# Seven-product weight chunks in the swiglu stages from chunk 3 on instead of chunk 4

## What is computed

```python
D_MODEL = 1024; SEQ = 512; DEPTH = 2; D_FF = 2816

def swiglu_ffn(x, wi, wo):
    gate, up = jnp.split(x @ wi, 2, axis=-1)
    return (jax.nn.silu(gate) * up) @ wo

for l in range(DEPTH):
    x = layer_norm(alpha * x + 0.5 * swiglu_ffn(x, ffn1_wi[l], ffn1_wo[l]), ln_g[l, 0], ln_b[l, 0])
    mix = even_mixer(x, ...) if l % 2 == 0 else odd_mixer(x, ...)
    x = layer_norm(alpha * x + mix, ln_g[l, 1], ln_b[l, 1])
    x = layer_norm(alpha * x + 0.5 * swiglu_ffn(x, ffn2_wi[l], ffn2_wo[l]), ln_g[l, 2], ln_b[l, 2])
```

## Time and profile before

| | before |
|---|---|
| median of 3 runs | 3608.43 us (3606.93 to 3611.15) |
| profiled execution, its own time | 3602.56 us |
| its span, first to last instruction | 3600.8 us |
| TensorE busy | 3516.6 us, 98% |
| VectorE busy | 2192.2 us, 61% |
| ScalarE busy | 1556.2 us, 43% |
| GpSimd busy | 476.4 us, 13% |
| mean granted TensorE clock | 0.994 |

### The profile page before, as it was taken

How to read it: one execution, slowest core, us unless ns; L and a number is a source line. 1 busy time by engine, 2 the same in 40 slices (tenths; PEclk the granted TensorE clock), 3 DMA queues, 4 the chain that set the end, 5 groups by cost and what they waited for, 6 DMA issues and landing times. The chain is left out here.

```text
span 3600.8 us, 55748 instructions
## 1 busy us (share of the span) xinstructions
PE 3516.6 (98%) x21468; PEld 3045.0 (85%) x21468; DVE 2192.2 (61%) x3419; ACT 1556.2 (43%) x2472; POOL 476.4 (13%) x443
## 2 busy tenths in 40 slices
PE   8999999999999999989999999999999999999998
PEld 7998877998899888678998887878888878888887
DVE  6963566895489445655895445656662545556643
ACT  4542544553355343543554333445442323454432
POOL 1022103002300230032102201011111000021110
PEclk9999999999999999999999999999999999999999
DMA  3232221233322322121223333222222333132222
GB/s 141 105 127 96 89 82 66 99 105 119 115 101 106 119 99 94 67 83 48 95 104 124 111 111 120 88 97 92 95 86 97 128 108 115 64 112 94 93 92 84
DMA packets 66513, 357.45 MB, mean 99 GB/s; under 512 B 7185, under 2 KB 16929, under 8 KB 37409
## 3 DMA queue, kind: packets, MB, share of 16 engines
q1 hardware_dynamic: 62368, 342.45, 26.8%
q0 software_dynamic: 3968, 12.59, 1.1%
HBM read 341.37 MB, written 13.63 MB: 99 GB/s over the span
## 5 line engine op out<-in xcount | busy, mean ns | idle before, releaser
L394 DVE TENSOR_TENSOR w_lo<-raw,w_hi 128x2048 fp32r<-128x2048 f32 (+2 forms) x233 | 482.5, 2071 | 600.6 <-ACT w_hi L389 584.6
L389 ACT ACTIVATE w_hi<-raw 128x2048 fp32r<-128x2048 f32 (+2 forms) x224 | 373.5, 1668 | 700.3 <-PE bank L432 596.5
L430 PE MATMUL bank<-x_hi,w_hi 128*128 128x512 f32 (+1 forms) x1344 | 522.6, 389 | 2.0 <-DVE w_lo L394 2.0
L431 PE MATMUL bank<-x_lo,w_hi 128*128 128x512 f32 (+1 forms) x1344 | 510.8, 380 | 0.0
L432 PE MATMUL bank<-x_hi,w_lo 128*128 128x512 f32 (+1 forms) x1344 | 510.7, 380 | 0.0
L430 PE MATMUL banks<-x_hi,w_hi 128*128 128x512 f32 (+1 forms) x832 | 323.5, 389 | 18.2 <-POOL x_lo L628 10.9
L431 PE MATMUL banks<-x_lo,w_hi 128*128 128x512 f32 (+1 forms) x832 | 318.0, 382 | 0.0
L432 PE MATMUL banks<-x_hi,w_lo 128*128 128x512 f32 (+1 forms) x832 | 317.8, 382 | 0.0
L430 PEld LDWEIGHTS bank<-x_hi,w_hi 128*128 128x128 f32 x1344 | 253.6, 189 | 64.5 <-issue 15.4
L430 PE MATMUL bank<-f_g_hi,w_hi 128*128 128x512 f32 (+1 forms) x792 | 294.2, 371 | 3.3 <-POOL f_g_lo L1338 3.3
L432 PEld LDWEIGHTS bank<-x_hi,w_lo 128*128 128x128 f32 x1344 | 253.5, 189 | 48.1
(11 more groups left out here) (595 smaller groups left out, 8326.4 us busy)
## 6 DMA issues: line engine op xcount, KB each, us to landing
raw<-in_weights SPq DMA_DIRECT2D x217, 1024.0 KB, 4.8
raw<-in_weights SPq DMA_DIRECT2D x96, 704.0 KB, 4.0
X<-x_kept SPq DMA_DIRECT2D x5, 2048.0 KB, 9.6
x_kept<-X SPq DMA_DIRECT2D x6, 1024.0 KB, 4.7
raw<-in_weights SPq DMA_DIRECT2D x8, 768.0 KB, 4.3
odd_arena<-in_kv SPq DMA_DIRECT2D x8, 512.0 KB, 3.6
x_kept<-X SPq DMA_DIRECT2D x2, 2048.0 KB, 12.7
work<-in_rpb POOLq DMA_DIRECT2D x12, 256.0 KB, 3.0
```

The source lines that it names most:

```text
L389: act.activation(w_hi[:, s, 0:size], raw[:, s, 0:size], ACT.Copy).then_inc(hi_ready.sem, 1)
L394: dve.tensor_tensor(w_lo[:, s, 0:size], raw[:, s, 0:size], w_hi[:, s, 0:size].bitcast(F32), ALU.subtract).then_inc(lo_ready.sem, 1)
L430: pe.matmul(out, wh[:, w], hi(k), start=first and n == 0, stop=False, skip_group_check=not group)
L431: pe.matmul(out, wh[:, w], lo(k), start=False, stop=False, skip_group_check=not group)
```

## The change

`S0` goes from 4 to 3: chunk 3 of each swiglu stage becomes a block chunk and is no longer split and multiplied whole. The block parts change slots and PSUM sides with it (`u` of the first block chunk is 1). The hand-written start is arranged anew on ScalarE and VectorE: the low parts of the first block chunk stand between those of T, and the combinations q = 1, 2, 3 of the first block chunk between its last low parts (`begun=True` leaves them out of `body`). Chunks 4 and 5 move partly into the loops, which begin one step earlier. In the last chunk, all seven parts go to one slot with a simpler rule, and three high parts are made ahead of the half silus.

```diff
-                S0, LATE = 4, 10
+                S0, LATE = 3, 10
-                LAST_SLOT = (3, 0, 1, 2, 3, 0, 1)
...
                 def weight_block(w, j, q):
-                    if is_last(j):
-                        return w[:, other, LAST_SLOT[q] * 512:LAST_SLOT[q] * 512 + 512]
                     at = q % 4 * 512
-                    return w[:, own if q < 4 else other, at:at + 512]
+                    return w[:, other if q < 4 or isinstance(j, int) and j == FT - 1 else own, at:at + 512]
...
-                            if j == 3:
-                                pe.wait_ge(product_ready.sem, product_ready.at(1))
...
                         gate_up(1, 0)
-                        gate_up(1, 1)
-                        blocks_of(S0, 0)
-                        blocks_of(S0 + 1, 1)
-                        with pe.Fori(3, FT // 2 - 1) as i:
+                        blocks_of(S0, 1)
+                        with pe.Fori(2, FT // 2 - 1) as i:
...
                             if j is S0:
-                                act.wait_ge(chunk_used.sem, PRIME + n0 + (3 if q < 4 else 4))
-                            elif is_last(j):
-                                if q >= 4:
-                                    act.wait_ge(block_used.sem, used_of(j, q - 4))
-                                elif q == 3:
-                                    act.wait_ge(chunk_used.sem, j + (PRIME + n0))
-                                elif q > 0:
-                                    act.wait_ge(block_used.sem, used_of(j - 1, q + 3))
+                                act.wait_ge(chunk_used.sem, PRIME + n0 + (2 if q < 4 else 3))
+                            elif isinstance(j, int) and j == FT - 1 and q >= 4:
+                                act.wait_ge(block_used.sem, used_of(j, q - 4))
...
-                        def body(j, u, v, early, more=True):
+                        def body(j, u, v, early, more=True, begun=False):
                             for q in range(7):
-                                combine(j, u, q, g)
+                                if not (begun and q < 4):
+                                    combine(j, u, q, g)
                                 block_low(j + 1, v, q)
...
                         rest(0, 1)
-                        split(1, 0)
...
-                        sums(S0, 0, range(4))
+                        sums(S0, 1, range(3))
                         low_g(0, 0)
-                        t_split(3, 1)
+                        block_low(S0, 1, 0)
+                        t_split(2, 1)
+                        block_low(S0, 1, 1)
                         t_split(1, 2)
+                        block_low(S0, 1, 2)
+                        t_split(3, 3)
+                        block_low(S0, 1, 3)
+                        sums(S0, 1, (3,))
+                        t_split(4, 5)
+                        block_low(S0, 1, 4)
                         rest(1, 0)
+                        combine(S0, 1, 1, None)
+                        block_low(S0, 1, 5)
+                        combine(S0, 1, 2, None)
+                        block_low(S0, 1, 6)
+                        combine(S0, 1, 3, None)
                         low_g(1, 1)
...
-                        sums(S0 + 1, 1, (3,))
-                        low_g(2, 0)
-                        body(S0, 0, 1, True)
-                        body(S0 + 1, 1, 0, True)
-                        with dve.Fori(3, LATE // 2) as i:
+                        sums(S0 + 1, 0, range(4))
+                        body(S0, 1, 0, True, begun=True)
+                        with dve.Fori(2, LATE // 2) as i:
```

More of the change, by code:

```diff
@@ L875, in whole_bank @@
                 def whole_bank(j):
-                    return (0, 2, 4, 0)[j]
+                    return (0, 2, 4)[j]
                 def used_of(j, q):
@@ L1066, in copy_first, with t_high @@
                             act.activation(U1, region(u, 0), ACT.Copy).then_inc(first_copied.sem, 1)
-                        def t_high(q):
+                        def t_high(n, q):
                             act.wait_ge(t_raw.sem, t_raw.at({1: 3, 2: 1, 3: 2, 5: 4}[q]))
@@ L1097, in _ @@
                             silu_of(1, 1)
-                            split(1, 0)
+                        block_high(S0, 1, 0)
                         round_g(1, 1)
-                        t_high(2)
-                        t_high(3)
-                        t_high(1)
-                        silu_of(2, 0)
[L1104 to L1109, removed]
+                        t_high(1, 2)
+                        t_high(2, 1)
+                        block_high(S0, 1, 1)
+                        t_high(3, 3)
+                        block_high(S0, 1, 2)
+                        block_high(S0, 1, 3)
+                        t_high(4, 5)
+                        silu_of(2, 0)
                         for q in (4, 5, 6):
-                            block_high(S0, 0, q)
-                        body(S0, 0, 1, True)
-                        body(S0 + 1, 1, 0, True)
-                        with act.Fori(3, LATE // 2) as i:
+                            block_high(S0, 1, q)
+                        body(S0, 1, 0, True)
+                        with act.Fori(2, LATE // 2) as i:
                             for u in range(2):
@@ L1124, in _ @@
                         copy_first(j, 0)
+                        for q in (1, 2, 3):
+                            block_high(j + 1, 1, q)
                         half_silu(j, 0, 1)
-                        block_high(j + 1, 1, 1)
-                        block_high(j + 1, 1, 2)
                         half_silu(j, 0, 0)
-                        block_high(j + 1, 1, 3)
                         block_high(j + 1, 1, 4)
@@ L1272, in _ @@
                         dve.tensor_tensor(T4R, T4R, T2R, ALU.subtract).then_inc(t_raw.sem, 1)
-                        sums(S0, 0, range(4))
+                        sums(S0, 1, range(3))
                         low_g(0, 0)
-                        t_split(3, 1)
+                        block_low(S0, 1, 0)
+                        t_split(2, 1)
+                        block_low(S0, 1, 1)
                         t_split(1, 2)
-                        rest(1, 0)
-                        low_g(1, 1)
-                        block_low(S0, 0, 0)
-                        block_low(S0, 0, 1)
-                        block_low(S0, 0, 2)
-                        t_split(2, 3)
-                        block_low(S0, 0, 3)
-                        t_split(4, 5)
-                        sums(S0 + 1, 1, (0, 1, 2))
-                        rest(1, 1)
-                        for q in (4, 5, 6):
-                            block_low(S0, 0, q)
-                        sums(S0 + 1, 1, (3,))
-                        low_g(2, 0)
-                        body(S0, 0, 1, True)
-                        body(S0 + 1, 1, 0, True)
-                        with dve.Fori(3, LATE // 2) as i:
+                        block_low(S0, 1, 2)
[4 more added lines that the diff above has]
+                        block_low(S0, 1, 4)
+                        rest(1, 0)
+                        combine(S0, 1, 1, None)
[3 more added lines that the diff above has]
+                        combine(S0, 1, 3, None)
+                        low_g(1, 1)
+                        sums(S0 + 1, 0, range(4))
+                        body(S0, 1, 0, True, begun=True)
+                        with dve.Fori(2, LATE // 2) as i:
                             for u in range(2):
@@ L1301, in _ @@
                         j = FT - 2
-                        block_low(j + 1, 1, 0)
                         for q in range(7):
                             combine(j, 0, q, g_plain[:, FT + j, :])
-                            if q >= 4:
-                                block_low(j + 1, 1, q - 3)
+                            if q < 4:
+                                block_low(j + 1, 1, q)
                         j = FT - 1
```

2 lines of the change are left out of this document (removed).

## The result

The changed kernel took 3626.58 us (median of 5 runs, 3625.13 to 3627.86); the kernel before, in the same comparison, 3608.43 (5 runs, 3602.68 to 3611.15). The ratio is 1.0054, with a 95% interval of 1.0041 to 1.0067: 15 to 24 us slower. The profiled executions are 3627.86 and 3602.56 us, 25.3 apart (spans 3626.1 and 3600.8).

What follows compares the result with a forecast made beforehand. TensorE bounds the stretch narrowly; after the change VectorE's queue would: 4 x 4.7 = 18.8 us, with the clock 21.1, takes 3602.56 to 3623.7, and the median 5.9 above to 3630 us (own range 3623 to 3636; 8 in 10: 3619 to 3637).

Steps and rivals of the forecast that it cites:

- What bounds the kernel: Swiglu stretch from T3: TensorE bounds it before with little to spare; after the change VectorE's queue does.
- VectorE's count: From T3 to the end of chunk 4's second combination: 33.4 us of VectorE work without a pause, each stage 4.7 later.
- The stalls: TensorE waits at product 5 of chunk 3 (0.4 us), product 0 of chunk 4 (1.8), its products 4 and 5 (3.4).
- TensorE's 0.80: Chunk 3 as 84 half-width matmuls for 48 full ones: 0.80 us less in each of four stages, if nothing waits.
- ScalarE, DMAs, last chunk at nothing: ScalarE's work, weight loads and the last chunk's new order add nothing; last chunk 0.3 us per stage either way.
- Chunk 6's landing: Chunk 6's load takes 4.8 us and lands as its first sum starts: nothing, up to 0.5 us per stage.
- The clock: Clock falls behind the stall at products 4 and 5 in one or two of four stages: 2.3 us, bounds 0 and 6.
- the own stalls of the kernel before: Product 5 waits in two other stages, 0.8 us in all; a late load might stall TensorE again.
- The rival by which the backlog goes on: Block chunks behind: late loads stall TensorE again, 0.5 to 1.5 us more per stage, 3632 to 3641 us; chance 18%.
- The baseline: Profiled execution of 3602.56 us becomes 3623.7 for its like; the median of the runs lies 5.9 above it, 3630.
- The rule on the pause between VectorE instructions: Next VectorE instruction starts only when the pipe is empty: 4.3 us more per stage, near 3647 us; given no chance.

Runs made afterwards that it cites:

- e8: Changed kernel with low parts 0 to 3 of chunk 3 cut from 512 to 32 columns, that computation left out; 3620.01 us, 1.0035 of the kernel before.
- e6: Changed kernel with low parts 0 and 1 of chunk 3 done twice, each time waited for; 3630.70 us, 1.0061 of the kernel before.
- e9: Kernel before with four low parts of chunk 4 cut from 512 to 32 columns, that computation left out; 3606.74 us, 0.9999 of the kernel before.
- e11: Changed kernel with all seven low parts of chunks 3 and 4 cut from 512 to 32 columns; 3601.06 us, 0.9982 of the kernel before.
- e4_plain_order: Changed kernel without interleaving: combinations 1 to 3 of chunk 3 again behind its low parts and chunk 4's sums; 3631.69 us, 1.0066 of the kernel before.

## Why the prediction was right, and where it was off

**What bounds the kernel: right.** VectorE's list from T3 on sets the end; e8 and e6 show it with a slope of one, e9 and e11 from the other side. One remark of the prediction does not follow from its rows: that the trace names VectorE and not TensorE as the busier engine for this stretch. Before, TensorE was busy for all of its 21.52 us and VectorE for 20.84. What decided was the work that the change adds to VectorE's list, and not which engine was busier before.

**VectorE's count: right.** 33.4 us to the end of combination 2 predicted; it ends at 685.83 + 0.41, 33.50 us after T3. The distance was 33.56 for 33.55, the stage 4.70 later for 4.7. That the distance agrees to the hundredth is luck: the list is 0.1 us longer than predicted, and TensorE went on 0.06 us after its end instead of 0.15. VectorE didn't idle.

**The stalls: right in place and size.** 0.34 for 0.4 at product 5 of chunk 3, 1.71 for 1.8 at product 0 of chunk 4, 0.57 + 2.77 for 3.4 at its products 4 and 5.

**TensorE's 0.80: right**, and hidden; e11 brought it out.

**ScalarE, DMAs, last chunk at nothing: right** as far as the trace tells. Chunk 6's landing, feared for up to 0.5 us, made VectorE wait 0.25 us in the second stage and cost TensorE nothing visible; from chunk 6 to the down product both kernels run at the same pace.

**The clock: a chance term, off in both directions.** A fall in one or two stages, 2.3 us, was entered. In the profiled execution three came, 4.2 us. By medians the change cost 3626.58 - 3608.43 = 18.15 us, of which the stalls make 17.5 (4 x 4.70 - 1.3), so that 0.65 us are left for the clock. Both lie within the bounds of 0 and 6. Why the medians show less of it than the profiled pair stays open: falls outside the stages differ from execution to execution, and only one of each kernel has a trace.

**A term was missing.** The prediction said of the own stalls of the kernel before only that they might come back (0.8 us in all). They went away instead, 1.3 us with the slow starts behind them. The rival by which the backlog goes on had the sign wrong. In the kernel before VectorE had waited 1.24 and 0.80 us for weights ahead of these stalls, and in the changed one it had no such wait; why the loads come in time there is not shown.

**The baseline.** The sum gave 3623.7 for the like of the profiled execution, which took 3627.86, and 3629.5 for the median, which was 3626.58. The profiled execution of the kernel before was faster than all five runs of its comparison, and that of the changed kernel the slowest of its five, so the two profiles lie 25.3 us apart and the medians 18.15. Against the median the forecast is 2.9 us too high: 1.3 by the missing term and 1.6 by the clock; rounding to 3630 added 0.5. It came out inside the own range of 3623 to 3636, and what carries it is VectorE's count.

**The rule on the pause between VectorE instructions** would have made the distance 37.9, an estimate; 33.56 was measured, so the rows decided rightly. The prediction gave the rule without its exception: the Trainium skill's "VectorE: DVE Perf Modes", The DRAIN you can't avoid, adds that a next instruction that is not held starts earlier. The trace agrees with that: 0.605 us from start to start at a duration of 0.69.

## What to carry to other kernels

Where an engine with 60% of the span goes last, count its list over one stretch, between two events of the order, at start-to-start prices; that gave each stall within 0.1 us. Making the busiest engine's work shorter pays nothing where another's list is already level with it: first look for what that list can lose. And before handing a list's parts to GpSimd, look where VectorE's operands lie: with both in SBUF, whichever engine comes second waits for the other's instruction to end.

## What the runs showed of the hardware

- A VectorE instruction with two SBUF operands that starts beside a GpSimd one ends after it: 1.44, 1.76 and 2.20 us for 0.69, 0.69 and 1.23. With an operand in PSUM it keeps its 0.41 us. GpSimd is held in turn (2.08 us for 1.29). Handing over a part of 0.605 us cost VectorE 0.55 to 1.07.
- Equal stalls don't give equal clocks: behind 2.77 us of standing still the granted clock was 0.58 for 3 us in one stage and 1.00 in another of the same execution; behind 5.9 us it was 0.50 in four stages of four (e4_plain_order).
- A VectorE instruction of 32 columns took 0.18 us and started the next after 0.10; one of 512 columns 0.69 and 0.605.
